# Where four slabs of unrelated matmuls stand in an RWKV stage: two at its head and one in each of two blocks, or one in each of four blocks

## The reference, cut to what matters

```python
def step(S, xs):
    rt, wt, kt, vt, kkt, at = xs
    S = (S * jnp.exp(wt)[:, :, None, :]
         - jnp.einsum('bhvk,bhk->bhv', S, kkt)[..., None] * (kkt * at)[:, :, None, :]
         + vt[..., None] * kt[:, :, None, :])
    return S, jnp.einsum('bhvk,bhk->bhv', S, rt)
```

## Time and profile before

| | |
|---|---|
| time, median of 3 runs | 1651.45 us (1650.85 to 1653.16) |
| time of the profiled execution | 1644.45 us |
| its span, first to last instruction | 1642.7 us |
| mean granted TensorE clock | 0.894 of full |
| PE busy | 1432.9 us (87%) |
| DVE busy | 805.8 us (49%) |
| ACT busy | 393.8 us (24%) |
| PE's part of the chain that ended last | 67% |
| compression matmuls (L1166), all 16 rows of both layers | 126.2 us busy |

### The profile page before, as it was taken

How to read it: one execution, slowest core, us unless ns; L and a number is a source line. 1 busy time by engine, 2 the same in 40 slices (tenths; PEclk the granted TensorE clock), 3 DMA queues, 4 the chain that set the end, 5 groups by cost and what they waited for, 6 DMA issues and landing times.

```text
span 1642.7 us, 28656 instructions
## 1 busy us (share of the span) xinstructions
PE 1432.9 (87%) x9928; PEld 1025.3 (62%) x9928; DVE 805.8 (49%) x2010; ACT 393.8 (24%) x765; POOL 170.1 (10%) x310
## 2 busy tenths in 40 slices
PE   5998989898898996678999899998989899776795
PEld 3774877887864674344458468778877448633542
DVE  1445547656553186552125366566663525756410
ACT  4230102111111243351241211032211113425300
POOL 0000000000000134440000000000000003344200
PEclk9987899988799996798999779899977999778898
DMA  7132321510022243557142333213100505363621
GB/s 298 66 105 70 135 80 59 174 52 2 1 106 90 95 127 110 182 188 286 52 168 67 104 103 118 65 54 128 52 1 1 194 1 153 102 203 107 242 80 64
DMA packets 92932, 175.95 MB, mean 107 GB/s; under 512 B 14082, under 2 KB 79795, under 8 KB 86899
## 3 DMA queue, kind: packets, MB, share of 16 engines
q1 hardware_dynamic: 80066, 124.58, 22.6%
q0 software_dynamic: 12720, 49.54, 8.6%
HBM read 161.27 MB, written 21.12 MB: 111 GB/s over the span
## 4 chain that ended last, share of the span: by engine, by line
PE 67%; DVE 13%; issue 11%; POOLq 3%; DMA 3%; ACT 1%; POOL 1%; SPq 0%; DVEq 0%; ACTq 0%
PE bank L562 15%; PE bank L599 12%; PE bank L1166 8%; PE bank L2669 3%; POOLq L386 3%; PE bank L495 2%; PE bank L795 2%; PE bank L1207 1%; DMA stream<-in_slcV 1%; DVE area L1668 1%; PE bank L1319 1%; DVE area L1705 1%; PE bank L565 1%; PE bank L803 1%; POOL stream L392 1%
## 5 line engine op out<-in xcount | busy, mean ns | idle before, releaser
L562 PE MATMUL bank<-stream,hT 128*128 128x512 f32 (+3 forms) x768 | 264.0, 502 | 14.6 <-ACT area L575 14.1
L599 PE MATMUL bank<-hT,stream 128*128 128x272 f32 x960 | 227.1, 398 | 5.1 <-DVE area L1551 5.1
L562 PEld LDWEIGHTS bank<-stream,hT 128*128 128x128 f32 x768 | 147.5, 195 | 115.7 <-issue 101.7
L599 PEld LDWEIGHTS bank<-hT,stream 128*128 128x128 f32 x960 | 183.7, 193 | 43.7 <-DVE area L1551 5.3
L1166 PE MATMUL bank<-stream,prm 128*128 128x256 f32 x512 | 126.2, 409 | 0.4 <-DVE YT L1532 0.4
L2669 PE MATMUL bank<-stream,YT 128*128 128x512 f32 x256 | 112.6, 601 | 4.8 <-DVE YT L2575 4.8
L1166 PEld LDWEIGHTS bank<-stream,prm 128*128 128x128 f32 x512 | 104.8, 207 | 18.0 <-issue 1.6
L2669 PEld LDWEIGHTS bank<-stream,YT 128*128 128x128 f32 x256 | 48.9, 192 | 66.1 <-issue 60.8
L2328 ACT ACTIVATE area<-area 128x256 f32<-128x256 f32 (+3 forms) x96 | 52.2, 544 | 139.8 <-DVE area L2625 138.2
L392 POOL DMA_DIRECT2D stream<-in_slcV x128 | 71.1, 557 | 84.8 <-PE bank L2066 22.9
L392 POOL DMA_DIRECT2D stream<-in_slcK x128 | 68.5, 536 | 108.6 <-PE bank L2210 35.4
(11 more groups left out here) (612 smaller groups left out, 2338.0 us busy)
## 6 DMA issues: line engine op xcount, KB each, us to landing
stream<-in_cmpL SPq DMA_DIRECT2D x256, 128.0 KB, 2.3
stream<-in_win_ SPq DMA_DIRECT2D x12, 2048.0 KB, 7.7
stream<-in_slcK SPq DMA_DIRECT2D x128, 64.0 KB, 2.2
stream<-in_slcK POOLq DMA_DIRECT2D x128, 64.0 KB, 2.4
stream<-in_slcV SPq DMA_DIRECT2D x128, 64.0 KB, 2.1
stream<-in_slcV POOLq DMA_DIRECT2D x128, 64.0 KB, 2.4
stream<-in_wout SPq DMA_DIRECT2D x4, 2048.0 KB, 8.8
out_winpast<-in_winraw POOLq DMA_DIRECT2D x2, 4064.0 KB, 25.0
```

The source lines that it names most:

```text
L562: last = nc.tensor.matmul(ps[:, 0:w], hT[:, k, tok(i)], ws[:, k, :], start=(k == 0), stop=(k == KT - 1))
L599: last = nc.tensor.matmul(ps[:, 0:HALF], ws[:, k, 128 * f:128 * f + 128], hT[:, k, HALF * s:HALF * s + HALF], start=(k == 0), stop=(k == K ...
```

## The change

All four compressions of stage R now stand in the same place, one in each block: row 4 in block 0, row 5 in block 1, row 6 in block 2, row 7 in block 3. None is left in the head. Matmuls, DVE instructions and transfers are the same in number and size, and the order of SP's list is unchanged.

```diff
@@ pe_r @@
-            pe_compress(pe, l, 4)
             pe.wait_ge(dve_done, at("LW", l))
             pe_r_turn(pe, l, 0)
             pe_r_sums(pe, l, 0)
             pe_project_rows(pe, l, "F2", 2)
-            pe_compress(pe, l, 5)
             for m in range(4):
@@ pe_r_solve @@
-                if lev == 3 and m < 2:
-                    pe_compress(pe, l, 6 + m)
+                if lev == 3:
+                    pe_compress(pe, l, 4 + m)
                 pe.wait_ge(dve_done, at("Z", l, m, lev))
@@ dve_r @@
                     dve(nc.vector.tensor_scalar(AG, AG, 0.5, 0.5, ALU.mult, ALU.add).then_inc(dve_done, 1))
-                    dve_compress(dve, l, 4)
                     dve_r_front(dve, l, 0, 0)
...
             dve.name("fm", l, 0)
-            dve_compress(dve, l, 5)
             for m in range(4):
@@ dve_r_block @@
                 elif lev == 3:
-                    if m < 2:
-                        dve_compress(dve, l, 6 + m)
+                    dve_compress(dve, l, 4 + m)
                     dve_r_ahead(dve, l, m + 1, 4)
```

## The result

The changed kernel is slower by about half a percent. Over 20 executions of each, the median went from 1652.89 to 1658.97 us, +6.1; the ratio is 1.0062 with a 95% interval of 1.0040 to 1.0083. Both are small against the spread of single executions, 1634 to 1664 us before and 1650 to 1670 after. (The medians are over all executions, the ratio over those in the chip's faster state alone, so the ratio says a little more.) The profiled execution took 1654.63 us, its span is 1652.6 (before 1642.7), PE was busy 1439.4, DVE 806.4 and ACT 393.9 us, and the mean granted clock was 0.892 (before 0.894).

What follows compares the result with a forecast made beforehand. In stage R, PE and DVE alternate: DVE waits for compression 4 in the head, PE for DVE in blocks 2 and 3. -9.4 + 2.6 + 12.1 - 1.7 = +3.6 us a layer, +7.2 for two: 1651.45 becomes 1658.7, range 1648 to 1667.

Steps and rivals of the forecast that it cites:

- Head, -9.4: Head of stage R: without its two compressions, block 0's products start 9.4 us sooner after `AG`, per layer.
- the bounds: Limits on the gap's price: 0 if the clock holds, about 4 us if also half during F2 and past first squarings.
- Gap ahead of block 0, +2.6: PE idles before block 0's products, which then start at half clock: 2.6 us more per layer.
- Blocks 2 and 3, +12.1: Added compressions in level 3 and their DVE instructions lengthen distances between additions of levels 2 to 4: +12.1 us per layer.
- Clock given back in the ends, -1.7: Level 4's addition to next block's first product, blocks 2 and 3: compressions may hold the clock, -1.7 us per layer.
- Blocks 0 and 1, 0: Each keeps one compression, only of another row, with the same two DVE instructions: 0 us.
- Transfers, 0: T2, T3, T4 wait for later row uses, but their 7.7 us to landing is covered by a whole block: 0.
- The rival in which the clock pays for everything: Compressions hold the clock in blocks 2 and 3, head gap doesn't drop it: -5 us in all, 1646.4; chance 0.12.
- The one in which the gap is free: Head gap costs no clock, the rest as forecast: +2.0 us in all, 1653.5, no change; chance 0.18.

Runs made afterwards that it cites:

- slab_front: Against the kernel before: only row 4's compression in the head, ahead of the wait for `LW`; rows 5, 6, 7 in blocks 0, 1, 2; 1664.14 us, ratio 1.0104.
- fill: The changed kernel plus 8 useless matmul instructions in the gap behind F2; 1661.97 us, ratio 1.0100 to the kernel before.
- halves_late_pad: Kernel before with half compressions in all blocks, their DVE instructions behind the copy of `yy`, 2 useless matmuls after each level 4 product; 1624.59 us, ratio 0.9857.

## Why the prediction was right

The forecast was +7.2 us, 1658.7, between 1648 and 1667; 1658.97 was measured, +6.1. By its steps:

- **Head, -9.4.** -8.8 and -7.9 in the two layers. The order of causes was right: L1604 starts 5.83 us behind `AG` where L1608 started 12.43 behind it, 6.6 sooner with ACT's lateness in it, as forecast. What was missed is F2, 9.19 us instead of 7.50, with the clock at 0.59 from 272 to 276. It made DVE wait 0.66 us. The two short waits ahead of F2 were named, but the half clock in F2 stood among the bounds and not in the sum. The Trainium skill ("TensorE: Matmul & The Clock Gate", "HAM oscillation — how this bites in real kernels") tells of waits for transfers between bursts of matmuls. It doesn't speak of waits as short as the 1.12 and 0.83 us here, so these rows go beyond it and don't confirm it.
- **Gap ahead of block 0, +2.6.** +1.2 and +1.3 (first mask 4.26 and 4.31 us behind the first product, 3.04 before). The products didn't start at half clock, as forecast: the clock was 1.00 through the gap and to 285.5, and about half from there to 289. In slab_front, where the clock fell inside the gap, it cost the 2.6. Head and gap together give -7.6 and -6.6, where the sum had -6.8.
- **Blocks 2 and 3, +12.1.** Distances of 8.77 and 8.67 for 8.80, 3.09 and 3.73 for 3.09 and 3.73. Right to 0.2 us in layer 0; in layer 1 the same distances grew by 12.8.
- **Clock given back in the ends, -1.7.** In layer 0 the ends of blocks 2 and 3 took 6.89 and 6.64 us instead of 7.06 and 8.86, -2.4; in layer 1 5.34 and 8.86 instead of 8.87 and 6.62, -1.3.
- **Blocks 0 and 1, 0.** This was the weak step. Their own order didn't change, but block 1's front part took 19.03 us in both layers instead of 15.3 and 15.4 (clock 0.57 over 318 to 330). In layer 0 a shorter end of block 1 (5.34 for 8.63) paid it back, in layer 1 nothing did. That is 3.3 of the 5.0 us between layer 1, which lost 6.0, and layer 0, which lost 1.0. Against it stands a gain that the sum didn't have either: block 2's front part was shorter by 1.5 and 2.5 us.
- **Transfers, 0.** No wait for T2, T3 or T4 shows.

One reading of the rows before was wrong. The stretch from 227 to 230.5 was taken as a clock lowered by a wait, and it isn't one: PE's wait there is 2.56 us and ends at 230.49, so it began at 227.9, and the clock was falling while PE was still busy.

```profile
225.00:227.00 2.00, 2.00 (x18) 2.00 (x17) 0.16 (x1) 0.00 (x0) 1.07 (x2) 0.88 0.08 14
```

So that a gap lowers the clock rested on no row of this kernel, and the 2.6 us came out at 1.2. slab_front shows it later: there the clock was 0.98 in the gap's first 3 us and 0.50 right behind it, over 290 to 294.

The path was right: head and level distances alone give +3.1 and +4.9 us in the two layers. That the mean of the two layers, +3.5, meets the +3.6 of the sum is luck in the clock's terms, which nearly cancel in this profile: the second profile of the same kernel has blocks 2 and 3 longer by 3.5 to 10.2 us and is 17.6 us longer in stage R. The parts on the path can be added up; the clock's part is a spread of some 20 us from one execution to the next. By the ratio the change costs some 10 us, by the medians 6, and the forecast's 7.2 lies between. Why it falls in one block's front part and not in the other's with the same instructions isn't settled.

The rival in which the clock pays for everything was refuted by the result. The one in which the gap is free was nearer than its chance of 0.18 says: fill took the gap's price away and won nothing.

## What to carry to other kernels

Before moving independent work out of one place into another, ask at both what the other engine is doing there: a slab of PE work costs its length minus the wait that it fills, here 2.8 us behind F2 and 5.4 in a block for a slab of 6.9. Ahead of `LW` it cost 4.5 to 5.3 and not its whole length, since the clock in F2 took part of it. Cutting it nearer to the size of the waits (half a slab in each block) was worth more than moving it. Take the unloading instructions of such a slab out of the chain as well: two DVE instructions of 0.7 us for each slab, moved behind the last addition, gave 4 and 9 us on the path, and 17 and 30 us in all with a clock that no sum foresaw. Where two engines take turns, look at the granted clock beside the waits, and compare kernels over many executions, since one profile's clock can hide or feign a whole term.

## What was not expected of the hardware

- With 1.5 us of useless matmuls in PE's wait near the end of each block (pad), the mean granted clock went from 0.887 to 0.910 and the time from ratio 1.006 to 0.988. More than half of the gain in the profile lies outside the stage that was padded.
- Without the slab ahead of the transposes, F2 took 9.19 to 9.61 us in every profile, with it 7.50.
- The time of one and the same program follows its mean granted clock to within some 5 us: 1670.25 us at 0.880, 1660.54 at 0.886, 1650.27 at 0.894 among 12 executions.
- Padding isn't a rule: in the head it moved the loss to the end of the same block (fill), and with half slabs the clock then fell in the following products of one layer (halves_late_pad).
